# A two-block mixer on one core: the order of scores and value products in a round of the local attention

## The reference, cut to what matters

```
def one_block(args):
    qn, kn, vn, mn = args
    s_loc = jnp.einsum('bqhgd,bkhd->bhgqk', qn, kn).astype(F32)
    s_loc = jnp.where(mn, s_loc, NEG_INF)
    s_ctx = jnp.einsum('bqhgd,bchd->bhgqc', qn, kc).astype(F32)
    s_sink = jnp.broadcast_to(sink_l[None, :, :, None, None], s_ctx.shape[:-1] + (1,))
    p = jax.nn.softmax(jnp.concatenate([s_sink, s_ctx, s_loc], axis=-1), axis=-1)
    ...
    return (jnp.einsum('bhgqc,bchd->bqhgd', p_ctx, vc)
            + jnp.einsum('bhgqk,bkhd->bqhgd', p_loc, vn))
```

## Time and profile before

| What | Value |
|---|---|
| Time, median of 3 runs (lowest, highest) | 3666.86 us (3666.4, 3673.7) |
| The profiled execution's own time | 3664.23 us |
| Its span | 3662.4 us |
| Mean granted clock of PE | 0.985 of full speed |
| PE busy | 3491.9 us, 95% of the span |
| DVE busy | 1863.2 us, 51% |
| ACT busy | 931.6 us, 25% |
| POOL busy | 1815.1 us, 50% |

### The profile page before, as it was taken

One profiled execution on the slowest core, in us unless ns is written; L12 is line 12 of the kernel. 1 busy time (PEld: TensorE's weight loads), 2 busy tenths in 40 slices (PEclk: granted clock), 3 DMA queues, 4 the chain that ended last, 5 costly groups with the idle time before them and its releaser, 6 DMA issues.

```text
span 3662.4 us, 49453 instructions
## 1 busy us (share of the span) xinstructions
PE 3491.9 (95%) x19612; PEld 2795.2 (76%) x19612; DVE 1863.2 (51%) x2551; ACT 931.6 (25%) x1503; POOL 1815.1 (50%) x1826
## 2 busy tenths in 40 slices
PE   5998997999899799999999999999999999999998
PEld 3786786778678677777788888876777778888886
DVE  5684825559481556335543444355434553443346
ACT  4113534321363433133211011113223221111111
POOL 3342014567302477547744445457745864444445
PEclk9999998999999899999999999999999999999999
DMA  5510010331001143213211111114322311111113
GB/s 211 213 52 12 2 37 25 107 124 58 18 2 43 39 153 127 65 51 118 89 48 43 55 52 38 58 44 138 99 57 74 122 55 55 48 39 58 48 37 100
DMA packets 87607, 257.57 MB, mean 70 GB/s; under 512 B 9808, under 2 KB 12880, under 8 KB 86608
## 3 DMA queue, kind: packets, MB, share of 16 engines
q1 hardware_dynamic: 70896, 216.65, 18.4%
q10 hardware_dynamic: 16480, 37.76, 3.5%
HBM read 229.20 MB, written 16.78 MB: 67 GB/s over the span
## 4 chain that ended last, share of the span: by engine, by line
PE 79%; DVE 11%; POOL 5%; ACT 2%; issue 1%; DMA 1%; SPq 0%; DVEq 0%; POOLq 0%; ACTq 0%
PE banks L683 22%; PE banks L685 21%; PE banks L684 21%; POOL w_lo L2428 4%; DVE wk L1920 3%; PE banks L799 2%; PE banks L813 2%; PE banks L832 2%; DVE nt L1825 1%; POOL w_hi L2425 1%; DVE wk L2076 1%; DVE h_lo L1838 1%; DMA gw<-w_mod 1%; PE banks L827 1%; DVE nt L1814 1%
## 5 line engine op out<-in xcount | busy, mean ns | idle before, releaser
L683 PE MATMUL banks<-h_hi,w_hi 128*128 128x512 f32 (+1 forms) x3488 | 1357.0, 389 | 14.4 <-POOLq L2433 13.2
L685 PE MATMUL banks<-h_hi,w_lo 128*128 128x512 f32 (+1 forms) x3488 | 1335.4, 383 | 0.0
L684 PE MATMUL banks<-h_lo,w_hi 128*128 128x512 f32 (+1 forms) x3488 | 1333.0, 382 | 0.0
L2428 POOL TENSOR_TENSOR w_lo<-raw,w_hi 128x256 fp32r<-128x256 f32 x1320 | 1270.0, 990 | 31.2
L2425 POOL CAST w_hi<-raw 128x1024 fp32r<-128x1024 f32 (+2 forms) x390 | 398.1, 1021 | 1641.1 <-PE banks L685 1179.7
L683 PEld LDWEIGHTS banks<-h_hi,w_hi 128*128 128x128 f32 x3488 | 655.4, 188 | 164.7 <-POOLq L2433 26.6
L684 PEld LDWEIGHTS banks<-h_lo,w_hi 128*128 128x128 f32 x3488 | 655.4, 188 | 136.5 <-issue 7.4
L685 PEld LDWEIGHTS banks<-h_hi,w_lo 128*128 128x128 f32 x3488 | 654.9, 188 | 134.3
L2373 DVE TENSOR_SCALAR nt<-wk,v 128x1024 f32<-128x1024 f32 x88 | 90.1, 1024 | 462.0 <-ACTq L1757 435.6
L1536 ACT ACTIVATE wk<-banks 128x512 f32<-128x512 f32 x200 | 118.9, 595 | 706.6 <-PE banks L685 681.5
L683 PE MATMUL banks<-g_hi,w_hi 128*128 128x512 f32 x704 | 280.4, 398 | 11.5 <-DVEq L2362 6.4
(11 more groups left out here) (232 smaller groups left out, 3409.7 us busy)
## 6 DMA issues: line engine op xcount, KB each, us to landing
raw<-w_in SPq DMA_DIRECT2D x118, 512.0 KB, 3.5
raw<-w_ffn SPq DMA_DIRECT2D x96, 512.0 KB, 3.5
raw<-w_out SPq DMA_DIRECT2D x64, 512.0 KB, 3.5
raw<-w_down SPq DMA_DIRECT2D x96, 256.0 KB, 2.6
x<-w_mod SPq DMA_DIRECT2D x16, 1024.0 KB, 7.0
wk<-residual ACTq DMA_DIRECT2D x42, 256.0 KB, 3.1
gw<-w_mod SPq DMA_DIRECT2D x4, 2048.0 KB, 20.5
residual<-x ACTq DMA_DIRECT2D x4, 2048.0 KB, 9.4
```

Source lines behind the costliest of these rows:

```text
L683: mm(o, wh[:, ws], hi[:, at_, t0:t0 + n], start=kt == 0, stop=False)
L684: mm(o, wh[:, ws], lo[:, at_, t0:t0 + n], start=False, stop=False)
L685: last = mm(o, wl[:, ws], hi[:, at_, t0:t0 + n], start=False, stop=kt == nk - 1)
L2428: last = G.tensor_tensor(w_lo[:, piece], raw[:, piece], w_hi[:, piece].bitcast(F32), ALU.subtract)
```

## The change

In each round of PE the scores of the pair three ahead are issued straight after the transposes of the round's pair, and the value products of the pair behind come after them.

```
                 for i in range(len(pairs)):
                     turn(i)
+                    if i + 3 < len(pairs):
+                        scores(i + 3)
                     if i:
                         weigh(i - 1)
-                    if i + 3 < len(pairs):
-                        scores(i + 3)
                 weigh(len(pairs) - 1)
```

## The result

The changed kernel takes 3769.53 us (median of 4 runs, 3766.26 to 3774.76) against 3669.81 for the kernel before in the same comparison. The ratio is 1.0277, with a 95% interval from 1.0263 to 1.0291: about 102 us slower. The profiled executions differ by as much: 3766.26 against 3664.23, spans 3764.5 against 3662.4.

The account below looks back on a forecast made before the run. PE was taken as the bound before; the change puts scores, value products, mix and masking in line, 5.63 us a full round. 97.5 us on the profiled 3664.2 gives 3761.7, plus 2.6 for the median: 3764, range 3745 to 3800.

Parts of the forecast that it names:

- The ring: Attention rounds: masking ends, then scores, value products, mix and masking follow in line, each waiting for the last.
- Its length: Full round with 5 key blocks: scores, value products, hand-over, mix and masking sum to 5.63 us, where 3.98 was taken.
- the mix until the masking: DVE in each round: from the mix's start until the next masking can start, 0.64 us.
- The clock over the rounds should read 1.00: PE in the attention rounds: sign that full clock holds although PE is busy only 3.98 of 5.63 us.
- a fall that would not last: PE in the rounds: at half clock about 8.0 of 8.2 us would be busy, so the clock would rise again.
- the sum of 97.5: Both layers' attention rounds: added time in us, from 52.7 + 45.7 = 98.4 less about 1 for the ends.
- Transposes and the clock: PE: the skill says transposes do not count alike as activity; the trace's rise from 2.50 to 1.35 us speaks against it.
- 2.82 us of DVE's part: PE's wait in a full round, in which the next pair's transposes (1.24 us) fit and cost nothing.
- The two copies: ACT's and DVE's copies of turned weights end before full value products; even with 2 key blocks, at most 2.4 us.
- DVE's wait at L2001: Mix in the rounds: waits for value products (L832) about 2.0 us a round, 120 to 130 in all.
- PE's wait at L799: Before the scores: rises from 39.3 to about 137 us, released by L1976, 1.6 us at full rounds.
- The rival that PE's waits could be won back: Attention rounds: earlier scores let DVE mask sooner, at most 27 us less, 3640; chance 0.02.

Follow-up runs that it names:

- the two by two: Either order on PE and on DVE, ratios to the kernel before: scores first on PE alone 1.0277, masking before mix on DVE alone 1.0299, both 1.0003.
- experiment 4: Changed kernel with 8 of each pair's transposes on PE done a second time: 3768.31 us, ratio 1.0278 to the kernel before.
- The last experiment: Kernel before with 20 and 12 identity transposes ahead of the second and third pair of scores of each layer: 3664.19 us, ratio 0.9993.
- experiments 4 and 5: 8 of each pair's transposes done twice, on the changed kernel (3768.31 us, ratio 1.0278) and on the kernel before (3728.59 us, ratio 1.0166).
- experiment 1: Changed kernel with masking of pair i+3 ahead of mix of pair i-1 on DVE: 3668.84 us, ratio 1.0003 to the kernel before.
- experiment 6: Changed kernel with one extra 128x336 copy on DVE in each mix, behind L2002: 3794.31 us, ratio 1.0347 to the kernel before.
- experiment 3: Changed kernel with the scores moved up once more, ahead of the same round's transposes: 3907.24 us, ratio 1.0658 to the kernel before.

## Why the prediction was right, point by point

**The ring.** Right, and shown: the chain lists its links, the two by two shows that it takes both orders to form it, transposes put into it add their own length to 0.01 us a round at full clock, and a copy put into its DVE part counts where it did not before.

**Its length.** 5.63 was predicted for a full round, 5.50 came. The term that was too large is the mix until the masking: 0.64 predicted, 459.80 - 459.26 = 0.54 measured. I had taken it from 437.61 to 438.25 in the earlier trace rows, where the masking was not held by the mix alone but by its scores as well, begun at 437.57 and 0.63 long: a wait was booked as work. The masking came out at 461.91 - 459.80 = 2.11 for 2.13, the rest agrees to 0.01. Over 64 rounds the 0.10 of the mix is 6.4 us too much. In layer 0 ten rounds were to take 50.66; at full clock throughout, in experiment 4, they take 49.83 (385.39 to 435.22). In layer 1 the same place comes again after 42.86 us, for 43.60 predicted, by the chain:

```profile
1068.67 1.13 PE banks L799 x8
...
1111.53 1.13 PE banks L799 x8
```

**The clock.** "The clock over the rounds should read 1.00" was wrong. In the windows of 60 us of layer 0 it reads less:

```profile
340.00:400.00 60.00, 45.20 (x416) 32.91 (x414) 34.30 (x130) 26.75 (x62) 0.00 (x0) 0.93 0.00 1
400.00:460.00 60.00, 44.17 (x430) 32.69 (x425) 32.92 (x126) 24.15 (x55) 0.00 (x0) 0.94 0.01 1
460.00:520.00 60.00, 42.71 (x423) 31.46 (x423) 34.73 (x132) 26.43 (x60) 0.00 (x0) 0.97 0.00 1
```

PE's timeline shows where it fell: on the small pairs, whose few transposes leave longer gaps, 1.9 to 2.2 us in layer 0 and 1.74 in layer 1.

```profile
430.23 0.66 PE L813 MATMUL banks<-cst,nt 128*128 128x128 f32 x4
432.80 2.20 PE L799 MATMUL banks<-wk 64*128 64x256 f32 x8 [1.91 <-DVE nt L1976]
...
436.95 0.66 PE L813 MATMUL banks<-cst,nt 128*128 128x128 f32 x4
439.79 2.36 PE L799 MATMUL banks<-wk 64*128 64x256 f32 x8 [2.18 <-DVE nt L1976]
```

From 432.80 to 439.79 is 6.99, where the same two places with the next pair of heads are 5.35 apart (485.74 and 491.09). One round in layer 1 and four in layer 0 are longer in this way, by 0.8 to 1.6 us, together 7.3. The prediction had named scores at 2.50 us in the rounds as a sign that it was wrong; four of the 64 groups come near it, with 2.20 to 2.46 us. The clock came back each time, within a round or two, as reckoned for a fall that would not last. So the rounds are 6.4 us shorter by the ring and 7.3 longer by the clock than the sum of 97.5, which makes 98.4. The two attentions grew by 99.1 us: from the first scores to the projection behind the last value products it is 208.56 and 177.75 us, where it was 154.18 and 133.05. The other 3.0 of the 102.1 lie in stretches that the change did not touch, among them the rotation of layer 1, whose four matmuls (L760) took 1.95 us before and 3.36 now; 3.0 us is also less than executions of one kernel differ by (3659.7 to 3675.3 for the kernel before). The closeness of 3764 to the measured 3769.53 is thus in part luck, two errors of opposite sign.

**Transposes and the clock.** The prediction set the rule of "TensorE: Matmul & The Clock Gate", Part 4: PE-mode transpose, in the Trainium skill, against the rise behind 8 transposes. The last experiment bears the trace out: with nothing but transposes in the gaps the scores took 1.35 us and not 2.50. Here float32 transposes of 128x128 act as work for the clock.

**What hides.** The transposes were predicted to be free behind 2.82 us of DVE's part; experiments 4 and 5 show it. The two copies never held the value products of full rounds; at L827 the copies of ACT are named 4 times for 1.3 us in all, and only before weight loads that follow scores with 2 key blocks, the case that the prediction called even; the matmuls there did not wait.

**The waits.** DVE's wait at L2001 was said to be 120 to 130 us and is 143.6. The falls of the clock are about half of the excess: without them, in experiment 4, it is 136.3. The rest is that a full round waits 2.19 us and not about 2.0. PE's wait at L799 was said to go from 39.3 to about 137, and the view says 216.4. That was a misreading of the earlier trace rows: it counts a standstill twice, for the loads and for the matmuls. Taken as matmuls alone it was 16.3 before and is 102.8. The rival that PE's waits could be won back, at up to 27 us, was priced too high for the same reason (of the 16.3, all but 4.3 are the waits ahead of the first rounds); experiment 1 gave it the earlier scores that it asked for, and it gained nothing.

## What to carry to other kernels

When two engines hand two kinds of work to and fro, follow each engine's order once around: a move on one side is harmless only if the other side takes the jobs in the same order. Before moving an instruction ahead, ask what now stands behind it, who waits for that, and whether that waiter stands ahead of the one who will release the moved instruction. Take a link's length from a place where nothing else holds the next step; a start that also waited for another engine gives a link that is too long.

## What the runs showed of the hardware that was not expected

Each kernel has one profiled execution. In that of the changed kernel the clock of TensorE fell on single rounds behind gaps of 1.7 to 2.2 us between short bursts, while full rounds of 5.50 us with one gap of 1.45 us ran at 2.4 GHz. In experiment 6 two of the falls came in full rounds, behind gaps of 1.70 us. With gaps of 2.70 us (experiment 3) it was at half speed in many rounds and up again in others of the same shape. A matmul behind four semaphore waits began 0.26 us after the end of the DVE instruction that released it (L2002, then L827), while scores behind one wait began 0.04 us after theirs; whether the number of waits makes the difference no run shows.
